# A two-layer hybrid backbone step on one core: router on scaled x ahead of the norm's root, shift added by diagonal products, expert gates moved behind the gather

## The reference, cut to what matters

```python
x = x + g1 * o                                  # o = the output projection
h = modulate(rmsnorm(x, n2), sh2, sc2)          # x * rsqrt(mean(x^2)+eps) * n2 * (1+sc2) + sh2
g_logit = h @ w_rg + b_rg                       # 4 groups
e_logit = h @ w_re + b_re                       # 16 experts
g_sel = argmax(g_logit); two best experts inside the group, their softmax times the group's
hid = silu(h @ w_gate[e]) * (h @ w_up[e]);  y = sum over the chosen e of gate * (hid @ w_down[e])
x = x + g2 * y
```

## Time and profile before

| | |
|---|---|
| median of 3 runs | 821.7 us (819.85 to 822.02) |
| the profiled execution | 819.76 us, span in the trace 817.9 us |
| PE / DVE / ACT / POOL busy | 758.9 (93%) / 586.0 (72%) / 476.9 (58%) / 49.7 us (6%) |
| mean granted TensorE clock | 0.984 |
| mean DMA rate | 227 GB/s |

### The profile page before, as it was taken

How to read it: one execution, slowest core, us unless ns; L and a number is a source line. 1 busy time by engine, 2 the same in 40 slices (tenths; PEclk the granted TensorE clock), 3 DMA queues, 4 the chain that set the end, 5 groups by cost and what they waited for, 6 DMA issues and landing times.

```text
span 817.9 us, 10722 instructions
## 1 busy us (share of the span) xinstructions
PE 758.9 (93%) x3980; PEld 571.8 (70%) x3980; DVE 586.0 (72%) x934; ACT 476.9 (58%) x768; POOL 49.7 (6%) x36
## 2 busy tenths in 40 slices
PE   4997989999989999999989998988997799999995
PEld 2565878457945888888766787745793688888874
DVE  4229676884558789999663866688544988999965
ACT  3033883575355777777542388357534687777752
POOL 0000641000000000000000064100000000000000
PEclk9999999999999999999999999999998999999998
DMA  9952032978347899999760113285830179999912
GB/s 368 422 186 75 30 128 60 419 294 310 104 155 308 289 374 358 372 363 370 270 273 12 58 46 129 104 339 177 303 109 0 52 268 377 357 376 371 360 51 80
DMA packets 33488, 185.98 MB, mean 227 GB/s; under 512 B 5136, under 2 KB 6288, under 8 KB 16400
## 3 DMA queue, kind: packets, MB, share of 16 engines
q1 hardware_dynamic: 33424, 185.16, 60.2%
HBM read 182.53 MB, written 2.62 MB: 226 GB/s over the span
## 4 chain that ended last, share of the span: by engine, by line
PE 79%; DVE 11%; ACT 5%; issue 4%; DMA 1%; DVEq 0%; SPq 0%; ACTq 0%
PE psum L739 22%; PE psum L854 11%; PE psum L768 11%; PE psum L1056 8%; PE psum L825 7%; PE psum L791 3%; PE psum L620 2%; PE psum L1070 1%; DVE att L1930 1%; PE psum L817 1%; PE psum L924 1%; PE psum L717 1%; PE psum L1026 1%; PE psum L661 1%; PE psum L752 1%
## 5 line engine op out<-in xcount | busy, mean ns | idle before, releaser
L1726 DVE TENSOR_TENSOR split<-ring,split 128x2048 fp32r<-128x2048 f32 x96 | 219.9, 2291 | 27.6 <-ACT split L1319 25.0
L1319 ACT CAST split<-ring 128x2048 fp32r<-128x2048 f32 x96 | 183.4, 1911 | 18.1 <-PE psum L768 14.5
L739 PE MATMUL psum<-split,y_hi 128*128 128x512 f32 x512 | 162.7, 399 | 0.0
L739 PEld LDWEIGHTS psum<-split,y_hi 128*128 128x128 f32 x512 | 93.7, 188 | 19.6
L739 PE MATMUL psum<-split,y_lo 128*128 128x512 f32 x256 | 100.6, 393 | 0.0
L854 PE MATMUL psum<-ring_r,hT_hi 128*128 128x512 f32 x216 | 74.0, 397 | 2.7 <-ACT qkT L1413 2.4
L768 PE MATMUL psum<-split,hidT 128*128 128x512 f32 x256 | 70.3, 396 | 1.8 <-DVE hidT_lo L1731 1.8
L825 PE MATMUL psum<-hT,ring 128*128 128x384 f32 x192 | 69.2, 499 | 0.0
L768 PEld LDWEIGHTS psum<-split,hidT 128*128 128x128 f32 x256 | 47.4, 187 | 14.5 <-DVE hidT_lo L1731 3.6
L2120 POOL TENSOR_TENSOR ud<-const,da_hi 128x1024 fp32r<-128x1024 f32 x12 | 30.7, 2578 | 431.8 <-DVE da_lo L1823 431.3
L739 PEld LDWEIGHTS psum<-split,y_lo 128*128 128x128 f32 x256 | 48.0, 188 | 11.1
(11 more groups left out here) (258 smaller groups left out, 1339.0 us busy)
## 6 DMA issues: line engine op xcount, KB each, us to landing
ring<-in_w_gu SPq DMA_DIRECT2D x64, 1024.0 KB, 5.0
ring<-in_w_ada SPq DMA_DIRECT2D x40, 1024.0 KB, 6.7
ring<-in_w_down SPq DMA_DIRECT2D x32, 1024.0 KB, 5.2
ring<-in_w_rows SPq DMA_DIRECT2D x12, 1024.0 KB, 5.1
ring<-in_first SPq DMA_DIRECT2D x8, 1024.0 KB, 14.7
ring<-in_w_out SPq DMA_DIRECT2D x8, 1024.0 KB, 4.8
ring<-in_w_xbc SPq DMA_DIRECT2D x8, 784.0 KB, 8.4
par<-in_par SPq DMA_DIRECT2D x1, 1632.0 KB, 11.9
```

What stands on the lines that cost most here:

```text
L739: last = pe.matmul(dst, x[:, g, t, :], w[:, j, :], start=(t == 0 and i == 0), stop=(t == KD - 1 and i == 2))
L1319: act.copy(splits[n % SPLITS][:, 0, :], slot(key)).then_inc(raised("whi", l, p), 1)
L1726: tt(lo, slot(unit_key(l, p, n)), hi.bitcast(F32), ALU.subtract).then_inc(raised("wlo", l, p), 1)
```

## The change

It reorders and rewrites the stretch between the output projection and the first expert in both layers.

1. ACT makes, with each square, also `aT` = x times the scale (two activations a chunk). The router multiplies `aT`, not the finished h: `aT` is the stationary operand (128 columns) and the 20 router columns move, 3 matmuls for each of 8 chunks. The logits come out with tokens as rows, so the 20x384 copy and its turn are gone. DVE multiplies by the reciprocal root of each token (`rtok`) and adds a bias that holds the shift's share (`shift_bias`: DVE forms shift times router weights during `wout`, PE sums it with ones).
2. The sum of squares is also taken as a column for each token tile (9 more one-column matmuls). ACT computes `rtok` from the columns, and `std`, the root itself, from the rows.
3. h in rows is aT turned, plus the shift: PE turns `aT` and adds `std` times a diagonal matrix of the shift into the same bank (`hshift`, 24 f32 matmuls of 128 columns, behind all transposes of its half). ACT builds the 16 diagonals in `wout`. `h_hi` and `h_lo` are scaled by `rtok` as they are written, now without a stride.
4. The rows are made in halves of the features; `hrow`, `hshift`, `h_hi`, `h_lo` for the second half stand behind `rank` and the last `ada` steps. In layer 0, 4 `ada` steps come first of all, ahead of the router and the sums; before, 3 stood behind the sums.
5. ACT copies 12 of the gather's 16 outputs, DVE 4. `combine` stands behind both halves of the gather, `ada_turn` (layer 0) between the gather and `combine`. `selT` has a step of its own ahead of the first expert, `cwT` and `cwg` go behind the third product, and the gate product of expert 0 (`hid`) follows them.
6. `norm` of the second kind no longer runs on DVE. The host lays out `w_gate` and `w_up` with other rows in a partition, at the same size.

```diff
-    s = [("select", p), ("split", p, 0), ("gather", p), ("split", p, 1), ("weights", p), ("split", p, 2)]
+    s = [("select", p)] + split(0) + [("gather", p, 0)] + split(1) + [("gather", p, 1)] + [("combine",)] * once + split(2) + [("turn_sel", p)]
+    s += [("gua", p, 0), ("split_hi", p, 3), ("split_lo", p, 3), ("gub", p, 0), ("split_hi", p, 4)]
+    s += [("gua", p, 1), ("weights", p)] + [("flag",)] * once + [("hid", p, 0), ("split_lo", p, 4), ("turn_hid", p, 0)]
+    s += behind("gua", 1) + [("gub", p, 1), ("hid", p, 1)] + behind("gub", 1) + [("down", p, 0)] + behind("down", 0)
...
-    s += [("turn_mix",)] + ada[14:] + [("ada_turn", l, 2), ("wsplit", 1), ("wout",), ("norm", 1)] + ahead[:3]
-    s += [("router",), ("hrow", 0), ("rank",), ("hrow", 1), ("hrow", 2), ("h_lo",)] + ahead[3:] + [("flag",)]
+    s += [("turn_mix",)] + ada[14:] + [("ada_turn", l, 2), ("wsplit", 1), ("wout",)] + ahead[:4]
+    s += [("shift_bias",)] + [("router", c) for c in range(3)] + [("norm", 1)] + [("router", c) for c in range(3, KD)]
+    s += [("hrow", m, 0) for m in range(TILES)] + [("hshift", m, 0) for m in range(TILES)]
+    s += [("h_hi", m, 0) for m in range(TILES)] + [("logits",), ("h_lo", 0, 0), ("rank",)] + ahead[4:]
+    s += [("hrow", m, 1) for m in range(TILES)] + [("hshift", m, 1) for m in range(TILES)]
+    s += [("h_lo", 1, 0), ("h_lo", 2, 0)] + [("h_hi", m, 1) for m in range(TILES)] + [("h_lo", m, 1) for m in range(TILES)]
+    experts = moe_steps(0)
     if ahead:
-        s.append(("ada_turn", l + 1, 0))
-    return s + [("combine",)] + moe_steps(0) + [("more",)]
+        at = experts.index(("gather", 0, 1)) + 1
+        experts[at:at] = [("ada_turn", l + 1, 0)]
+    return s + experts + [("more",)]
...
+                for c in (0, KD - 2, KD - 1):
+                    if c:
+                        pe.wait_ge(sig["sq"], KD * (2 * l + n) + c + 1)
+                    if n:
+                        for m in range(TILES):
+                            pe.matmul(dst[:, TOK + m:TOK + m + 1], sq[:, c, m * P:(m + 1) * P], ones[:, 0:1],
+                                      start=(c == 0 and m == 0), stop=(c == KD - 1), skip_group_check=True)
...
-                    pe.wait_ge(*fill(("cwT", l, p)))
+                    pe.wait_ge(*fill(("cwT", l, p), 6))
...
-                    pe.wait_ge(*fill(("cwg", l, p)))
+                    pe.wait_ge(*fill(("cwg", l, p), 0))
...
                     elif kind == "router":
+                        c = arg[0]
...
+                        pe.wait_ge(sig["scaled"], per["scaled"] * l + c + 1)
                         for m in range(TILES):
+                            last = pe.matmul(dst[:, m * n:(m + 1) * n], aT[:, c, m * P:(m + 1) * P], wr[:, l, c, :],
+                                             start=(c == 0 and m == 0), stop=(c == KD - 1), skip_group_check=True)
...
+                    elif kind == "hshift":
+                        m, half = arg
+                        dst = bank(("hrow", l, m, half))
+                        pe.wait_ge(*taken(("ss", l, 1)))
+                        for j in range(4):
+                            last = pe.matmul(dst[:, j * P:(j + 1) * P], std[:, m * P:(m + 1) * P],
+                                             diag[:, 1 if m else 0, 4 * half + j, :], start=False, stop=True,
+                                             skip_group_check=True)
...
+            def row_norm(l):
+
+                key = ("ss", l, 1)
+                act.wait_ge(*full(key))
+                src = bank(key)
+                act.activation(rtok, src[:, TOK:TOK + TILES], ACT.Ln, bias=eps_col, scale=1.0 / D).then_inc(act_step, 1)
+                act.wait_ge(act_step, act_steps())
+                act.activation(rtok, rtok, ACT.Exp, scale=-0.5).then_inc(sig["rtok"], 1)
+                act.activation(src[:, 0:TOK], src[:, 0:TOK], ACT.Ln, bias=eps_col, scale=1.0 / D).then_inc(act_step, 1)
+                act.wait_ge(act_step, act_steps())
+                act.activation(std, src[:, 0:TOK], ACT.Exp, scale=0.5).then_inc(*was_read(key))
...
                         out_hi(l, 2)
+                        act.wait_ge(*taken(("adaT", l, 1)))
+                        for j in range(2):
+                            for c in range(KD):
+                                act.activation(diag[:, j, c, :], c_("ident"), ACT.Copy, scale=mods[:, l, SH2 + c, j:j + 1])
                         squares(l, 1, range(0, 3))
                         out_hi(l, 3)
```

More of the change, by code:

```diff
@@ L642, in sums @@
                 pe.wait_ge(sig["fold"], 2 * l + n + 1)
[L643 to L646, removed]
+                for c in (0, KD - 2, KD - 1):
[5 more added lines that the diff above has]
+                                      start=(c == 0 and m == 0), stop=(c == KD - 1), skip_group_check=True)
+                    last = pe.matmul(dst[:, 0:TOK], ones, sq[:, c, :], start=(c == 0 and not n), stop=(c == KD - 1),
+                                     skip_group_check=True)
                 last.then_inc(*filled(key))
@@ L680, in moe @@
             def moe(l, kind, arg):
-                if kind == "weights":
+                if kind == "turn_sel":
+                    p = arg[0]
+                    for g in range(NG):
+                        pe.wait_ge(*fill(("selT", l, p, g)))
+                        dst = bank(("selT", l, p, g))
+                        for m in range(TILES):
+                            last = pe.transpose(dst[:, m * P:(m + 1) * P], sel[:, m, g, :].bitcast(F32), ident)
+                        last.then_inc(*filled(("selT", l, p, g)))
+                elif kind == "weights":
                     p = arg[0]
                     pe.wait_ge(sig["cw"], per["cw"] * l + 1)
-                    pe.wait_ge(*fill(("cwT", l, p)))
+                    pe.wait_ge(*fill(("cwT", l, p), 6))
                     dst = bank(("cwT", l, p))
@@ L1062, in _ @@
                                 last.then_inc(out_spent, 1)
+                    elif kind == "shift_bias":
+                        pe.wait_ge(sig["shift_wr"], per["shift_wr"] * l + 1)
+                        pe.wait_ge(*fill(("shift_bias", l)))
+                        pe.matmul(bank(("shift_bias", l))[:, 0:2 * (NG + NE)], ones, shift_sum.rearrange("p j n -> p (j n)"),
+                                  start=True, stop=True).then_inc(*filled(("shift_bias", l)))
                     elif kind == "router":
+                        c = arg[0]
@@ L1064, in _ @@
                         n = NG + NE
[L1065 to L1070, removed]
-                                             start=(k == 0), stop=(k == KD - 1))
-                        last.then_inc(*filled(("logitsT", l)))
@@ L1752, in _ @@
                     if kind == "norm":
[L1753 removed]
+                        if not arg[0]:
+                            norm(l, 0)
                     elif kind == "ada_turn":
```

233 lines of the change are left out of this document (127 added, 106 removed).

## The result

The changed kernel takes 839.5 us (median of 4, 835.3 to 841.6), the kernel before, run beside it, 820.8 (819.0 to 822.0): ratio 1.022, interval 1.018 to 1.027. Run again beside other kernels it took 836.3 (6 runs, 835.8 to 837.9), ratio 1.018 (1.015 to 1.021). It is slower, as forecast, but 839.5 lies outside the range of 819 to 836, and 18.7 us more is two and a half times the 7.5 that the sum gave. The profiled execution took 835.3 us and its span is 833.4, against a span of 817.9 before.

What follows compares the result with a forecast made beforehand. PE bounds the experts and nearly all of layer 0's stretch; layer 1 has some PE time to give. Layer 0 +7.4, layer 1 -1.9, clock +2.0 on 819.8 give 827.3, forecast 829.0 as median, range 819 to 836.

Steps and rivals of the forecast that it cites:

- the sum: Whole kernel: layer 0 +7.4, layer 1 -1.9, clock +2.0, together +7.5 us on the profiled execution's 819.8.
- the two waits: Ahead of the first product PE waits for selT's bank; in expert 0 serial gate work adds 3.2 us a layer.
- The clock: One half-clock stretch behind PE's idle time ahead of the first product in each layer, 1.0 us each, between 0 and 2.2.
- Work up to the gather: From last output product, PE ends last; gather starts at 26.2 us in layer 0 and 18.7 in layer 1.
- The price of 0.112 us: Cost of every new router, column-sum, bias and hshift pass on PE, taken from a row moving 64 columns.
- The rival of cheaper narrow passes: Narrow passes cheaper than the 64-column row; at 0.06 us they give back 12.2, total 817; chance 0.14.
- The wait ahead of the first product: Between gather and first product, PE idle 4.7 and 3.4 us for selT copies; first product 4.2 later, 5.1 earlier.
- the rival without a wait: Bank free, first products start at 39.0 and 31.1; takes off 7.2 and the clock's 2.0, about 820; chance 0.14.
- Inside expert 0: Between third product and turn, cwT, cwg, their copies and hid add 3.2 us a layer, PE idle in half.
- The diagonals and the new DVE work: Behind the output projection's cover: cost 0, diagonals at most 1.6 us a layer; DVE's new operations have microseconds of slack.
- more half clock: Rival: narrow router, sums and transposes bring one more half-clock stretch per layer, 1.7 us each; 832.5, up to 836; chance 0.22.
- the step from that execution to the median: Whole kernel: the median of the runs lies 1.9 us above the profiled execution, so 827.3 becomes the forecast 829.0.

Runs made afterwards that it cites:

- the wide router: Changed kernel, but router weights stationary again and 384 columns of aT moving, 16 passes in place of 48, result copied and turned: 833.6 us, ratio 1.015.
- The bank run: Changed kernel, but selT's four outputs go to banks 0 to 3 in place of the next ones in turn: 832.8 us, ratio 1.016.
- the run at full clock: Changed kernel with router weights stationary again and 384 columns of aT moving, plus unused 128x512 passes in PE's three waits: 828.1 us, ratio 1.010.
- run 12: Not a run number: the words are "wide-router run" and "12 turns". That run: changed kernel with the wide router, 833.6 us, ratio 1.015.

## Why the prediction was right and wrong

- **Direction and the two waits: right.** Slower, through a wait for selT's bank and the serial gates in expert 0. The clock is the third part, and it is wrong in size and place (below).
- **Work up to the gather: right.** At the full clock (the wide router, whose passes were to cost as much) the gather of layer 0 starts at 26.3 us (forecast 26.2), of layer 1 at 18.8 (18.7; 19.8 with my 1.0 of wait). In the changed kernel itself, with its clock, it starts at 28.8 and 21.3. The price of 0.112 us held: 18 router passes in 1.99 us. The rival of cheaper narrow passes falls.
- **The wait ahead of the first product: right.** Gather end to first product 6.3 us in layer 0 (forecast 6.4) and 4.6 in layer 1 (4.7). The bank run shows the cause; the rival without a wait falls.
- **Inside expert 0: nearly right.** From the first product to the down product the run at full clock has 14.8 us in layer 0, 3.3 more than before; the forecast had 3.2.
- **The diagonals and the new DVE work: right at nothing.** The output projection took 33.3 us as before, in both layers.
- **The clock: the step that failed.** The forecast said "I put one stretch at half clock behind each" of the two selT waits and took 1.0 us each, 2.0 in all. That term was to hold all of the clock, and it measured 9.6. The selT waits themselves were near their price: 1.5 us in layer 0, nothing in layer 1 of that trace. What failed is that two other places stood in the sum at nothing. The narrow passes before the gather cost 2.5 us a layer. The gates' wait cost 1.4 and 1.5, and it was priced without any half clock behind it, though it is made of two idle times and tiny passes between. The narrow router was left to a rival ("more half clock", 0.22), at 1.7 us a layer, though the earlier trace rows showed half clock behind such work in layer 0.
- **The range.** The median lies 3.5 us over its upper end of 836, which was the rival with one more place at 1.7 us a layer. With 9.6 for the clock the profiled execution comes out at 819.8 + 5.5 + 9.6 = 834.9, and it took 835.3. The rest is the step from that execution to the median, put at 1.9 and measured at 4.2. The three other executions had a mean clock of 0.969 to 0.973, this one 0.979, so they had more half clock; where, is open.
- **Small slips.** Layer 0's terms up to the gather add up to 26.1, not 26.2, and 827.3 + 1.9 is 829.2. They change nothing.

The Trainium skill (TensorE: Matmul & The Clock Gate, the table on what matters) asks for no gaps over about 3 us between bursts. For the selT wait this agrees: 4.58 us of idle brought the half clock in every trace, 3.3 in four of five. It doesn't cover the gates' wait, where PE was never idle for over 0.78 us at a time, nor the router, where it was not idle at all. The Trainium skill (the same page, Part 4) also says that transposes don't count as activity. No run here tests that for long: in the wide-router run 12 turns in a row took 1.5 us at clock 1.00, between other passes.

## What to carry to other kernels

Read the clock beside the busy share. Turning a product so that few columns move kept its busy time at full clock here (some 5.3 us for 48 passes at 0.111, 5.4 for the 16 wide ones) and still cost 2.5 us a layer in clock, on the router's later passes and on what followed. Price a new wait of PE at its idle time plus the slower products behind it (1.4 to 1.5 us here, when they came), even where tiny passes fill part of it. And when banks are handed out in turn, list who gets which bank after any added or removed step: one fixed bank here took away a wait of 4.6 us and made one of 1.5 at the other end of layer 1.

## What the runs showed that I had not expected

- PE busy for 6.00 of 6.00 us at clock 0.50, and 16.00 of 16.00 in the run with the ada steps spread: the router's passes of 20 columns, with the sums, turns and hshift around them, did not keep the clock up.
- 41 passes whose result nobody reads took 5 us off the median.
- The same program has its half-clock stretches in different places in two executions, also far from any edit (the mixer at 512 us, in the kernel before as well). A gain of 6.6 us in the rewritten stretches, less 1.8 at the kernel's end, showed as 0 to 3 us in the medians, and one trace alone would have told a wrong story of where it went.
